# Opening in quarters: x and the first weight chunk loaded, split and multiplied in four pieces on two queues; the first squares later

## The chip, the cores and the metric

The kernel runs on one NeuronCore of a Trainium2 chip. The metric is the device time of one execution in microseconds (us). Five engines work beside each other, each through its own list in order, and wait for one another by semaphores: TensorE (PE, matmuls), VectorE (DVE), ScalarE (ACT), GpSimd (POOL) and SyncE (SP, which here only issues DMAs). ScalarE and GpSimd can issue DMAs too; those of SP and of ScalarE go through two different queues.

## What is computed

Two transformer blocks on 256 tokens of width 1024, in fp32, one after the other. What the change touches is the very first step, the first feed-forward layer with its norm:

```python
def rms_norm(x, g):
    xf = x.astype(jnp.float32)
    r = lax.rsqrt(jnp.mean(xf * xf, axis=-1, keepdims=True) + NORM_EPS)
    return (xf * r).astype(x.dtype) * g

def swiglu(u, w_in, w_out):
    a, b = jnp.split(u @ w_in, 2, axis=-1)
    return (jax.nn.silu(a) * b) @ w_out
...
x = x + FFN_RES_WEIGHT * swiglu(rms_norm(x, ffn1_norm), ffn1_w_in, ffn1_w_out)
```

`ffn1_w_in` is 1024 x 5632. Behind this layer follow two attention mixers, a second such layer, a gated embedding, a short convolution, two squared-ReLU layers and a sparse attention, none of which the change touches.

## The kernel before

x is kept transposed as `h`, 8 tiles of 128 features x 256 tokens. All weights come from memory as 198 chunks of 128 x 2048 fp32 (1 MB each), which stream through a ring of three buffers `raw`. An fp32 product is made of fp32r parts: ScalarE copies a chunk to its high part `w_hi` (L418), VectorE subtracts to get the low part `w_lo` (L816); both lie in `w_hl`. The same is done with the operand x: `gained_hi` (L446) multiplies by the norm's gain and makes `x_h`, `gained_lo` (L866) makes `x_l`. `wide` (L1561) then makes a product of two matmuls: high weights with both parts of x (512 columns, L1564) and low weights with the high part of x (256 columns, L1565). `thirds` (L1567) does the same with three matmuls of 256 columns.

A chunk of `ffn1_w_in` holds 128 columns of a and 128 of b for all 8 tiles of x, so it takes PE 16 such pairs. Chunk j makes tile j of the hidden layer in two PSUM banks, and three pairs of banks take turns. The norm's factor 1/rms is not on the operand; it is applied to the results. So the products need only the gain, and the factor is made beside them: `square` (L467) on ScalarE, `sum_tiles` (L883) on VectorE, `sum_squares` (L1678) on PE, `mean_square` (L839) on VectorE, `rsqrt` (L449: logarithm and exponential) on ScalarE, `newton` (L848) on VectorE into `r_sb`.

For each tile j (`ups`, L481 on ScalarE and L919 on VectorE): ScalarE copies the second half of the two banks to `second` (L479), VectorE adds it to the first half as `t_ab` (`whole_up`, L916), multiplies a by the factor (L931) and by b (L933), ScalarE makes the sigmoid (L496), VectorE the product `hid_f` (L938), ScalarE its high part in `hidden` (L498) and GpSimd its low part (L369). VectorE's L938 of tile j waits until GpSimd has read `hid_f` of tile j-1. Between these, `nxt(c)` splits chunk c+3 into the ring place that chunk c has left: on ScalarE when PE has used chunk c, on VectorE behind that. SP loads chunk c+3 into `raw` when `w_lo` of chunk c is written (L344). PE's chunk j waits for `w_lo` of chunk j, and from j = 3 on for the `whole_up` of tile j-3 (L1701), whose banks it overwrites.

The opening is written out by hand. x comes in two halves of 512 KB with the gain `par` between them on SP's queue; chunk 0 comes in halves, the first on ScalarE's queue, the second on SP's; chunks 1 and 2 and the constants follow on SP's. Chunk 0 is split and multiplied in quarters (`up` with `first`, L1627), chunk 1 in halves (`up_halves`, L1649). Before the first product PE runs `WARM` = 25 matmuls on `zeros`; it starts them when four of GpSimd's memsets are done (L1735). Every engine executes its list in the order in which the code is written.

```python
            pe.wait_ge(setup, 4)
            for n in range(WARM):
                mm(bank[:, SUMS, :], zeros[:, 0:P], zeros[:, :], start=True, stop=True)
            feed_forward("ffn1", x_hl, 1)
```

Of the kernel before, what the change touches and what calls it, by code (L numbers as in the profile page):

```python
# [14 lines left out]
F32 = mybir.dt.float32  # L15
# [3 lines left out]
ALU = mybir.AluOpType  # L19
# [21 lines left out]
WARM = 25  # L41
# [101 lines left out]
def program(nc, x_t, p_t, positions, weights, small, consts, rel_bias, bias_rows, bias_skew, out):  # L143
    with ExitStack() as ctx:
# [55 lines left out]
        x_in, first_in = [sem(f"x_in{j}") for j in range(2)], sem("first_in")  # L200
# [128 lines left out]
        def _(sp):  # L329
            sp.dma_start(h[:, 0:4, :], x_t[:, 0:4, :]).then_inc(x_in[0], 16)  # L330
            sp.dma_start(par[:, 0:KT], small[:, 0:KT]).then_inc(gain_in, 16)
            sp.dma_start(h[:, 4:8, :], x_t[:, 4:8, :]).then_inc(x_in[1], 16)
            sp.dma_start(raw[:, 0, CH // 2:CH], weights[0, :, CH // 2:CH]).then_inc(raw_landed[0], 16)
# [75 lines left out]
        def _(act):  # L409
# [132 lines left out]
            act.dma_start(raw[:, 0, 0:CH // 2], weights[0, :, 0:CH // 2]).then_inc(first_in, 16)  # L542
            nc.scalar.preload_act_table_set("natural_log_exp_and_others")
            for half in range(2):
                act.wait_ge(x_in[half], 16)
                if half == 0:
                    act.wait_ge(gain_in, 16)
                if half == 0:
                    for j in range(2):
                        gained_hi(x_h[:, 2 * j:2 * j + 2, :], h[:, 2 * j:2 * j + 2, :], "ffn1", 2 * j, 2 * j + 2)  # L550
                    act.wait_ge(first_in, 16)
                for q in range(2 * half, 2 * half + 2):
                    if half == 1:
                        gained_hi(x_h[:, 2 * q:2 * q + 2, :], h[:, 2 * q:2 * q + 2, :], "ffn1", 2 * q, 2 * q + 2)
                        act.wait_ge(raw_landed[0], 16)
                    a = slice(512 * q, 512 * q + 512)
                    nc.scalar.activation(w_hi[:, 0, a], raw[:, 0, a], ACT.Copy).then_inc(first_hi if q < 3 else hi_split, 1)
# [11 lines left out]
            rsqrt("ffn1", load=False)  # L569
            nc.scalar.preload_act_table_set("sigmoid_and_others")  # L570
# [3 lines left out]
            nxt(1)  # L574
            ups("ffn1")
# [233 lines left out]
        def _(dve):  # L809
# [109 lines left out]
            def ups(stage):  # L919
# [112 lines left out]
            for half in range(2):  # L1032
                dve.wait_ge(x_in[half], 16)
                if half == 0:
                    for j in range(2):
                        operand_piece("ffn1", x_h, x_l, j)
                for q in range(2 * half, 2 * half + 2):
                    if half == 1:
                        operand_piece("ffn1", x_h, x_l, q)
                    a = slice(512 * q, 512 * q + 512)  # L1040
                    if q < 3:
                        dve.wait_ge(first_hi, q + 1)
                    else:
                        dve.wait_ge(hi_split, 1)
                    V.tensor_tensor(w_lo[:, 0, a], raw[:, 0, a], w_hi[:, 0, a].bitcast(F32),
# [1309 lines left out]
```

## Time and profile before

| | |
|---|---|
| median of 3 runs | 1201.18 us (1198.7 to 1201.41) |
| span of the profiled execution | 1197.3 us |
| PE busy | 1187.6 us (99%) |
| VectorE busy | 867.8 us (72%) |
| ScalarE busy | 646.7 us (54%) |
| GpSimd busy | 220.6 us (18%) |
| DMA | 217.53 MB, mean 182 GB/s |
| chain that ended last | PE 96%, DVE 2%, ACT 1%, DMA 1% |

The profile shows one execution. Its span goes from the first to the last instruction; the profile does not give that execution's device time apart, and the median of the runs is 3.9 us above the span. Busy times overlap, so their shares don't add up. A start time in the timeline is counted from the span's start. Matmuls overlap in the array: the distance between the starts of two tells their cost, not the length of one.

### The profile page before, as it was taken

The numbers are of one execution on the slowest core, as the hardware profiler recorded it, in microseconds if no ns is written. First come the engines' busy times: TensorE is split into PE (matmuls) and PEld (weight loads), VectorE is DVE, ScalarE is ACT, GpSimd is POOL, SyncE is SP. The second block draws the span as 40 slices with busy tenths as digits, with TensorE's granted clock in tenths as the row PEclk, the third lists the DMA queues.
The fourth block names the chain that finished last, engine by engine and source line by source line (L and its number), as shares of the span: only waits on it lengthen the run. The fifth ranks groups of instructions, "written<-read, shape, count | busy, mean of one in ns | idle before, by whom it ended". The sixth has DMA issues, their size and how long they took to land.

```text
span 1197.3 us, 19531 instructions
## 1 busy us (share of the span) xinstructions
PE 1187.6 (99%) x7802; PEld 1060.7 (89%) x7802; DVE 867.8 (72%) x1199; ACT 646.7 (54%) x868; POOL 220.6 (18%) x110
## 2 busy tenths in 40 slices
PE   9999999999999999999999999999999999999997
PEld 6888889988899888888999988888899878888886
DVE  6877767788868877766788786655579777766553
ACT  6655554465654755545643555543446784555441
POOL 0443301000000344310000025510000340554000
PEclk9999999999999999999999999999999999999999
DMA  8655555953345555555545555555576305555540
GB/s 315 213 178 195 191 177 182 285 201 107 106 150 181 179 204 179 200 186 189 177 160 179 193 199 203 179 206 177 192 265 246 107 2 178 209 181 205 179 174 36
DMA packets 31569, 217.53 MB, mean 182 GB/s; under 512 B 3584, under 2 KB 3856, under 8 KB 6272
## 3 DMA queue, kind: packets, MB, share of 16 engines
q1 hardware_dynamic: 30000, 210.33, 50.4%
q0 software_dynamic: 1344, 5.53, 1.6%
q8 instruction: 59, 0.97, 0.3%
q10 hardware_dynamic: 144, 0.52, 0.1%
q14 instruction: 22, 0.18, 0.0%
HBM read 215.30 MB, written 4.22 MB: 183 GB/s over the span
## 4 chain that ended last, share of the span: by engine, by line
PE 96%; DVE 2%; ACT 1%; DMA 1%; issue 0%; POOL 0%; DVEq 0%; ACTq 0%; SPq 0%; POOLq 0%
PE bank L1564 42%; PE bank L1565 21%; PE bank L1557 8%; PE bank L1558 7%; PE bank L1559 7%; PE bank L1965 1%; PE bank L1673 1%; DVE w_hl L816 1%; PE bank L1737 1%; PE bank L1675 1%; PE bank L1674 1%; DMA raw<-weights 1%; ACT w_hl L418 0%; PE bank L1859 0%; PE bank L1842 0%; PE bank L1878 0%
## 5 line engine op out<-in xcount | busy, mean ns | idle before, releaser
L816 DVE TENSOR_TENSOR w_hl<-raw,w_hl 128x2048 fp32r<-128x2048 f32 x194 | 444.1, 2289 | 116.5 <-ACT w_hl L418 115.5
L418 ACT ACTIVATE w_hl<-raw 128x2048 fp32r<-128x2048 f32 x195 | 370.6, 1903 | 113.8 <-PE bank L1565 65.5
L1564 PE MATMUL bank<-x_hl,w_hl 128*128 128x512 f32 x908 | 316.5, 395 | 0.0
L1564 PE MATMUL bank<-hidden,w_hl 128*128 128x512 f32 x832 | 288.6, 394 | 0.0
L369 POOL TENSOR_TENSOR hidden<-hid_f,hidden 128x256 fp32r<-128x256 f32 (+1 forms) x76 | 189.5, 2493 | 519.8 <-ACT hidden L501 307.0
L1565 PE MATMUL bank<-x_hl,w_hl 128*128 128x256 f32 x908 | 251.9, 277 | 0.0
L1565 PE MATMUL bank<-hidden,w_hl 128*128 128x256 f32 x832 | 230.5, 277 | 0.0
L1564 PEld LDWEIGHTS bank<-x_hl,w_hl 128*128 128x128 f32 x908 | 170.3, 188 | 39.6
L1564 PEld LDWEIGHTS bank<-hidden,w_hl 128*128 128x128 f32 x832 | 156.0, 188 | 36.2
L1565 PEld LDWEIGHTS bank<-x_hl,w_hl 128*128 128x128 f32 x908 | 170.6, 188 | 0.1
L479 ACT ACTIVATE second<-bank 128x512 f32<-128x512 f32 (+1 forms) x107 | 57.2, 535 | 199.1 <-PE bank L1565 199.0
L1564 PE MATMUL bank<-y_hl,w_hl 128*128 128x512 f32 x448 | 156.8, 396 | 0.0
L1565 PEld LDWEIGHTS bank<-hidden,w_hl 128*128 128x128 f32 x832 | 156.2, 188 | 0.0
L1557 PE MATMUL bank<-x_hl,w_hl 128*128 128x256 f32 x528 | 151.1, 286 | 0.1
L1558 PE MATMUL bank<-x_hl,w_hl 128*128 128x256 f32 x528 | 149.3, 283 | 0.0
L1559 PE MATMUL bank<-x_hl,w_hl 128*128 128x256 f32 x528 | 149.3, 283 | 0.0
L1565 PE MATMUL bank<-y_hl,w_hl 128*128 128x256 f32 x448 | 124.5, 278 | 0.0
L1557 PEld LDWEIGHTS bank<-x_hl,w_hl 128*128 128x128 f32 x528 | 101.2, 192 | 2.1 <-issue 1.2
L1564 PEld LDWEIGHTS bank<-y_hl,w_hl 128*128 128x128 f32 x448 | 84.0, 188 | 20.0 <-issue 0.3
L1558 PEld LDWEIGHTS bank<-x_hl,w_hl 128*128 128x128 f32 x528 | 101.3, 192 | 0.1
L1559 PEld LDWEIGHTS bank<-x_hl,w_hl 128*128 128x128 f32 x528 | 101.2, 192 | 0.0
L916 DVE TENSOR_TENSOR t_ab<-bank,second 128x512 f32<-128x512 f32 x76 | 52.5, 690 | 64.3 <-ACT second L479 64.2
(385 smaller groups left out, 1536.0 us busy)
## 6 DMA issues: line engine op xcount, KB each, us to landing
raw<-weights SPq DMA_DIRECT2D x197, 1024.0 KB, 4.9
bias_skew<-bias_rows POOLq DMA_DIRECT2D x1, 3072.0 KB, 26.0
gate_or_bias<-bias_skew POOLq DMA_DIRECT2D x1, 2048.0 KB, 9.6
h<-x_t SPq DMA_DIRECT2D x2, 512.0 KB, 6.0
out_t<-out_g SPq DMA_DIRECT2D x4, 256.0 KB, 2.5
con<-consts SPq DMA_DIRECT2D x1, 769.5 KB, 13.3
raw<-weights ACTq DMA_DIRECT2D x1, 512.0 KB, 5.2
raw<-weights SPq DMA_DIRECT2D x1, 512.0 KB, 7.9
```

The costliest lines, as they stand in the source:

```text
L369: nc.gpsimd.tensor_tensor(hidden[:, at, 1, :], src, hidden[:, at, 0, :].bitcast(F32), ALU.subtract).then_inc(hid_lo, 1)
L418: nc.scalar.activation(dst, src, ACT.Copy).then_inc(hi_split, 1)
L479: nc.scalar.activation(dst, src, ACT.Copy).then_inc(second_out, 1)
L816: V.tensor_tensor(w_lo[:, s, :], raw[:, s, :], w_hi[:, s, :].bitcast(F32), ALU.subtract).then_inc(lo_split, 1)
L916: V.tensor_tensor(t_ab[:, :, :], bank[:, s:s + 2, 0:S], second[:, j % 2, :, :], ALU.add).then_inc(ab_ready, 1)
L1557: mm(out_, w_hi[:, s, c:c + m], x[:, 0, :], start=start, stop=False, **kw)
L1558: mm(out_, w_hi[:, s, c:c + m], x[:, 1, :], start=False, stop=False, **kw)
L1559: return mm(out_, w_lo[:, s, c:c + m], x[:, 0, :], start=False, stop=stop, **kw)
L1564: mm(out_, w_hi[:, s, c:c + m], x, start=start, stop=False, **kw)
L1565: return mm(out_[:, 0:S], w_lo[:, s, c:c + m], x[:, 0, :], start=False, stop=stop, **kw)
L1673: mm(o, a, wh, start=first and n == 0, stop=False, **kw)
L1674: mm(o, a, wl, start=False, stop=False, **kw)
```

## The change

- x is loaded in four pieces of 256 KB on SP's queue, and chunk 0 in four pieces of 256 KB on ScalarE's queue, behind the gain, which moves there too. Chunks 1 and 2 follow x on SP's queue as before.
- ScalarE and VectorE work on x and chunk 0 piece by piece: the quarter of x, then the quarter of the chunk. Before, the first two pieces of x came ahead of the first quarter of the chunk.
- GpSimd sets `zeros` first. PE waits for that alone, runs 13 instead of 25 matmuls on zeros, and then waits for the other memsets.
- ScalarE makes the high part of chunk 2 ahead of the four squares, and both `second` of tile 1 and the high part of chunk 4 ahead of the logarithm, the exponential and the table load.
- VectorE makes the low part of chunk 2 ahead of the sums, and `whole_up` of tile 0 and the low parts of chunks 3 and 4 ahead of the mean square and `newton`. Chunk 4's low part stood behind `whole_up` of tile 1 before.
- PE sums the squares behind chunk 2 instead of chunk 1.
- `thirds` is gone; all pairs are `wide`.

VectorE's list from the sums to the second `whole_up`, before (`sq` are squares and sums, `t_m` the mean square, the three rows behind it up to `r_sb` are `newton`, `w_hl` of 128x2048 is a chunk's low part):

```order
L879 TENSOR_TENSOR sq<-sq 128x512 x3
L881 TENSOR_TENSOR sq<-sq 128x256
L816 TENSOR_TENSOR w_hl<-raw,w_hl 128x2048
L842 TENSOR_SCALAR t_m<-bank 128x256
L916 TENSOR_TENSOR t_ab<-bank,second 128x512
L816 TENSOR_TENSOR w_hl<-raw,w_hl 128x2048
L851 TENSOR_TENSOR t_a<-t_exp 128x256
L852 SCALAR_TENSOR_TENSOR t_a<-t_a,t_m 128x256
L854 SCALAR_TENSOR_TENSOR r_sb<-t_a,t_exp 128x256
```

The same place after the change:

```order
L810 TENSOR_TENSOR w_hl<-raw,w_hl 128x2048
L873 TENSOR_TENSOR sq<-sq 128x512 x3
L875 TENSOR_TENSOR sq<-sq 128x256
L910 TENSOR_TENSOR t_ab<-bank,second 128x512
L810 TENSOR_TENSOR w_hl<-raw,w_hl 128x2048 x2
L836 TENSOR_SCALAR t_m<-bank 128x256
L845 TENSOR_TENSOR t_a<-t_exp 128x256
L846 SCALAR_TENSOR_TENSOR t_a<-t_a,t_m 128x256
L848 SCALAR_TENSOR_TENSOR r_sb<-t_a,t_exp 128x256
```

Chunk 2's low part moved ahead of the sums, and those of chunks 3 and 4 now both stand ahead of the mean square.

ScalarE's list from chunk 1's high part to the first sigmoid, before (`second` is the copy from the banks, `t_a<-t_m` the logarithm, `t_exp<-t_a` behind it the exponential):

```order
L561 ACTIVATE w_hl<-raw 128x1024 x2
L468 ACTIVATE sq<-h 128x512 x4
L418 ACTIVATE w_hl<-raw 128x2048
L479 ACTIVATE second<-bank 128x512
L418 ACTIVATE w_hl<-raw 128x2048
L453 ACTIVATE t_a<-t_m 128x256
L454 ACTIVATE t_exp<-t_a 128x256
L570 ACT_TABLE_LOAD
L479 ACTIVATE second<-bank 128x512
L418 ACTIVATE w_hl<-raw 128x2048
```

And after:

```order
L555 ACTIVATE w_hl<-raw 128x1024 x2
L416 ACTIVATE w_hl<-raw 128x2048
L466 ACTIVATE sq<-h 128x512 x4
L477 ACTIVATE second<-bank 128x512
L416 ACTIVATE w_hl<-raw 128x2048
L477 ACTIVATE second<-bank 128x512
L416 ACTIVATE w_hl<-raw 128x2048
L451 ACTIVATE t_a<-t_m 128x256
L452 ACTIVATE t_exp<-t_a 128x256
L568 ACT_TABLE_LOAD
```

The logarithm and what hangs on it moved behind the copy of tile 1 and the high part of chunk 4.

```diff
-WARM = 25
+WARM = 13
...
         def _(sp):
-            sp.dma_start(h[:, 0:4, :], x_t[:, 0:4, :]).then_inc(x_in[0], 16)
-            sp.dma_start(par[:, 0:KT], small[:, 0:KT]).then_inc(gain_in, 16)
-            sp.dma_start(h[:, 4:8, :], x_t[:, 4:8, :]).then_inc(x_in[1], 16)
-            sp.dma_start(raw[:, 0, CH // 2:CH], weights[0, :, CH // 2:CH]).then_inc(raw_landed[0], 16)
+            for j in range(4):
+                sp.dma_start(h[:, 2 * j:2 * j + 2, :], x_t[:, 2 * j:2 * j + 2, :]).then_inc(x_in[j], 16)
...
-            for n, (t, value) in enumerate(((ones[:, :], 1.0), (zeros[:, :], 0.0), (v_pad[:, :, :], 0.0),
+            for n, (t, value) in enumerate(((zeros[:, :], 0.0), (ones[:, :], 1.0), (v_pad[:, :, :], 0.0),
...
-            act.dma_start(raw[:, 0, 0:CH // 2], weights[0, :, 0:CH // 2]).then_inc(first_in, 16)
+            act.dma_start(par[:, 0:KT], small[:, 0:KT]).then_inc(gain_in, 16)
+            for q in range(4):
+                a = slice(512 * q, 512 * q + 512)
+                act.dma_start(raw[:, 0, a], weights[0, :, a]).then_inc(first_in[q] if q < 3 else raw_landed[0], 16)
...
+            act.wait_ge(gain_in, 16)
+            for q in range(4):
+                act.wait_ge(x_in[q], 16)
+                gained_hi(x_h[:, 2 * q:2 * q + 2, :], h[:, 2 * q:2 * q + 2, :], "ffn1", 2 * q, 2 * q + 2)
+                act.wait_ge(first_in[q] if q < 3 else raw_landed[0], 16)
+                a = slice(512 * q, 512 * q + 512)
+                nc.scalar.activation(w_hi[:, 0, a], raw[:, 0, a], ACT.Copy).then_inc(first_hi if q < 3 else hi_split, 1)
...
+            split(2, 2, 1)
             for j in range(4):
                 square(j)
-            split(2, 2, 1)
...
             nxt(0)
-            rsqrt("ffn1", load=False)
-            nc.scalar.preload_act_table_set("sigmoid_and_others")
...
             nxt(1)
+            rsqrt("ffn1", load=False)
+            nc.scalar.preload_act_table_set("sigmoid_and_others")
...
-                    if c0 + j == 1:
-                        nxt(1)
...
+            split(2, 3)
             sum_tiles("ffn1")
-            split(2, 3)
-            mean_square("ffn1", bank[:, SUMS, 0:S])
             whole_up("ffn1", 0)
             nxt(0)
+            nxt(1)
+            mean_square("ffn1", bank[:, SUMS, 0:S])
             newton("ffn1", r_sb[:, :])
...
-                        form = thirds if half == 1 and t == 0 else wide
...
-                    if j == (1 if stage == "ffn1" else 0):
+                    if j == (2 if stage == "ffn1" else 0):
                         sum_squares(norm_no)
...
-            pe.wait_ge(setup, 4)
+            pe.wait_ge(setup, 1)
             for n in range(WARM):
                 mm(bank[:, SUMS, :], zeros[:, 0:P], zeros[:, :], start=True, stop=True)
+            pe.wait_ge(setup, 5)
```

## Rows read from the trace of the kernel before

**Rows 1.** The page: the span, and PE's busy time, share and instructions.

```profile
span 1197.3 us, 19531 instructions
...
PE 1187.6 (99%) x7802; PEld 1060.7 (89%) x7802; DVE 867.8 (72%) x1199; ACT 646.7 (54%) x868; POOL 220.6 (18%) x110
```

**Rows 2.** Timeline of the opening: start us, length us, engine, line, count [idle before <-releaser].

```profile
1.02 0.53 POOL L357 MEMSET zeros<- 128x512 bf16 x1
...
2.35 8.47 PE L1737 MATMUL bank<-zeros 128*128 128x512 bf16 x25 [2.35 <-POOL relb L357]
...
7.88 2.94 PE L1737 MATMUL bank<-zeros 128*128 128x512 bf16 x12
...
10.47 0.58 PE L1564 MATMUL bank<-x_hl,w_hl 128*128 128x512 f32 x1
```

**Rows 3.** SP's timeline, then issues of x, chunks 1, 1 and 2, 4: median to landing.

```profile
0.76 0.40 SPq L330 DMA_DIRECT2D h<-x_t  x1
...
2.62 1.00 SPq L335 DMA_DIRECT2D raw<-weights  x2
...
16.21 0.34 SPq L344 DMA_DIRECT2D raw<-weights  x1
...
h<-x_t SPq DMA_DIRECT2D x1, 512.0 KB, 5.1
...
raw<-weights SPq DMA_DIRECT2D x1, 1024.0 KB, 9.9
...
raw<-weights SPq DMA_DIRECT2D x2, 1024.0 KB, 10.9
...
raw<-weights SPq DMA_DIRECT2D x1, 1024.0 KB, 7.8
```

**Rows 4.** ScalarE's timeline: high parts of chunks 1 and 3, and the exponential.

```profile
12.58 2.01 ACT L561 ACTIVATE w_hl<-raw 128x1024 fp32r<-128x1024 f32 x2 [0.51 <-DMA raw<-weights]
...
20.80 1.92 ACT L418 ACTIVATE w_hl<-raw 128x2048 fp32r<-128x2048 f32 x1 [1.83 <-DMA raw<-weights]
...
23.36 0.42 ACT L454 ACTIVATE t_exp<-t_a 128x256 f32<-128x256 f32 x1
```

**Rows 5.** VectorE's timeline, from the last piece of x to chunk 6's low part.

```profile
11.58 0.88 DVE L866 SCALAR_TENSOR_TENSOR x_hl<-h,par,x_hl 128x256 fp32r<-128x256 f32 x2
...
13.68 2.36 DVE L1053 TENSOR_TENSOR w_hl<-raw,w_hl 128x1024 fp32r<-128x1024 f32 x2 [0.61 <-ACT w_hl L561]
15.95 2.14 DVE L879 TENSOR_TENSOR sq<-sq 128x512 f32<-128x512 f32 x3
...
22.45 0.42 DVE L842 TENSOR_SCALAR t_m<-bank 128x256 f32<-128x256 f32 x1 [1.64 <-PE bank L1681]
...
25.59 0.42 DVE L851 TENSOR_TENSOR t_a<-t_exp 128x256 f32<-128x256 f32 x1
...
28.29 0.69 DVE L916 TENSOR_TENSOR t_ab<-bank,second 128x512 f32<-128x512 f32 x1
...
32.60 0.42 DVE L938 TENSOR_TENSOR hid_f<-t_b,t_exp 128x256 f32<-128x256 f32 x1
...
36.45 2.29 DVE L816 TENSOR_TENSOR w_hl<-raw,w_hl 128x2048 fp32r<-128x2048 f32 x1
...
40.69 2.29 DVE L816 TENSOR_TENSOR w_hl<-raw,w_hl 128x2048 fp32r<-128x2048 f32 x1
```

**Rows 6.** PE's timeline: the first matmuls of chunks 1 and 5.

```profile
16.21 0.39 PE L1564 MATMUL bank<-x_hl,w_hl 128*128 128x512 f32 x1
...
38.90 0.40 PE L1564 MATMUL bank<-x_hl,w_hl 128*128 128x512 f32 x1
```

**Rows 7.** Tile hidden, 20 to 60 us: GpSimd's low part, ns min/median/max.

```profile
L369 POOL TENSOR_TENSOR hidden<-hid_f,hidden x8: 738/2274/2795, 29.0 to 59.4; 128x256 fp32r<-128x256 f32 x8
```

**Rows 8.** Windows at the tail: PE, PEld, DVE, ACT, POOL busy, granted clock, DMA.

```profile
1189.00:1191.00 2.00, 1.28 (x7) 0.66 (x7) 0.64 (x4) 0.86 (x4) 0.00 (x0) 1.00 0.00 0
...
1192.00:1193.00 1.00, 0.00 (x0) 0.00 (x0) 1.00 (x2) 0.00 (x0) 0.00 (x0) 0.84 0.00 0
```

More of the change, by code:

```diff
@@ L199, in program @@
         half_hi = sem("half_hi")
-        x_in, first_in = [sem(f"x_in{j}") for j in range(2)], sem("first_in")
+        x_in, first_in = [sem(f"x_in{j}") for j in range(4)], [sem(f"first_in{j}") for j in range(3)]
         gain_in, small_in, con_in, relb_in, pos_in, p_in = (
@@ L539, in gained_out @@
                 nc.scalar.activation(out_g[:, o, :], h[:, o, :], ACT.Copy, scale=col("final", o)).then_inc(gained, 1)
-            act.dma_start(raw[:, 0, 0:CH // 2], weights[0, :, 0:CH // 2]).then_inc(first_in, 16)
+            act.dma_start(par[:, 0:KT], small[:, 0:KT]).then_inc(gain_in, 16)
+            for q in range(4):
+                a = slice(512 * q, 512 * q + 512)
+                act.dma_start(raw[:, 0, a], weights[0, :, a]).then_inc(first_in[q] if q < 3 else raw_landed[0], 16)
             nc.scalar.preload_act_table_set("natural_log_exp_and_others")
[L544 to L557, printed above, removed]
+            act.wait_ge(gain_in, 16)
[5 more added lines that the diff above has]
+                nc.scalar.activation(w_hi[:, 0, a], raw[:, 0, a], ACT.Copy).then_inc(first_hi if q < 3 else hi_split, 1)
             act.wait_ge(raw_landed[1], 16)
@@ L1031, in _ @@
             dve.wait_ge(gain_in, 16)
[L1032 to L1045, printed above, removed]
-                                    ALU.subtract).then_inc(first_lo if q < 3 else lo_split, 1)
+            for q in range(4):
+                dve.wait_ge(x_in[q], 16)
+                operand_piece("ffn1", x_h, x_l, q)
+                a = slice(512 * q, 512 * q + 512)
+                if q < 3:
+                    dve.wait_ge(first_hi, q + 1)
+                else:
+                    dve.wait_ge(hi_split, 1)
+                V.tensor_tensor(w_lo[:, 0, a], raw[:, 0, a], w_hi[:, 0, a].bitcast(F32),
+                                ALU.subtract).then_inc(first_lo if q < 3 else lo_split, 1)
             for q in range(2):
@@ L1565, in wide @@
                 return mm(out_[:, 0:S], w_lo[:, s, c:c + m], x[:, 0, :], start=False, stop=stop, **kw)
-            def thirds(out_, s, c, m, x, start, stop):
-                kw = dict(skip_group_check=True)
-                mm(out_[:, 0:S], w_hi[:, s, c:c + m], x[:, 0, :], start=start, stop=False, **kw)
-                mm(out_[:, S:2 * S], w_hi[:, s, c:c + m], x[:, 1, :], start=False, stop=False, **kw)
-                return mm(out_[:, 0:S], w_lo[:, s, c:c + m], x[:, 0, :], start=False, stop=stop, **kw)
             def arrived(count):
@@ L1656, in up_halves @@
                     for t in range(2):
-                        form = thirds if half == 1 and t == 0 else wide
                         for k in range(KT // 2 * half, KT // 2 * (half + 1)):
-                            last = form(bank[:, 2 * slot + t, :], 1, k * 256 + t * P, P, x[:, k, :, :], k == 0,
+                            last = wide(bank[:, 2 * slot + t, :], 1, k * 256 + t * P, P, x[:, k, :, :], k == 0,
                                         k == KT - 1)
```

## The prediction

> **What bounds the kernel now.** I read the page first: TensorE (PE) is busy 1187.6 us of a span of 1197.3 us [rows 1]. The 9.7 us without it are the first 2.35 us and the tail, so from the first filler matmul on the kernel is one unbroken row of matmuls. Then I read the opening in the timeline. 25 matmuls on zeros run from 2.35 us, 0.425 us apart until about 8.3 us and 0.216 us apart after it (13 start before 7.88 us, 12 in the 2.59 us to 10.47 us); the first product starts at 10.47 us [rows 2]. The reader is to see that the fillers run right up to it: PE's start waits for their end. Chunk 1 starts at 16.21 us and chunk 5 at 38.90 us [rows 6], each 16 pairs of 0.346 us, or 5.54 us. So a microsecond saved at the start is saved at the end, if nothing between takes it back. What could take it is in rows 5: chunk 5's low part is written from 36.45 us for 2.29 us, to 38.74 us, and PE needs it at 38.90 us [rows 5, 6]. There the cover is 0.16 us.
>
> **The change, start of PE.** The memset of the zeros takes 0.53 us from 1.02 us, and PE now waits for two more behind it, until 2.35 us [rows 2]. As the first memset it ends at about 1.3 us, so PE starts at about 1.4 us. 13 fillers at the slow pace take 5.5 us and end at 6.9 us. The 12 removed ones are worth 2.6 to 5.1 us of PE.
>
> **First pieces.** The first 512 KB of x land 5.1 us after their issue at 0.76 us, at 5.9 us [rows 3]. A quarter holds half as much on each of the two queues: no row shows when it lands. It is bounded by 5.9 us above and by about 3.3 us below (half of the 5.1 us after the issue); I take 4.6 us, the middle. VectorE needs 0.88 us for the x of a piece and, at 2.36 us for two halves of a chunk, 0.6 us for its weights [rows 5]; ScalarE, ahead of it, takes much the same. That puts the first product at 4.6 + 0.9 (ScalarE, x) + 0.9 + 0.7 = 7.1 us, just behind the fillers. VectorE's 1.5 us for a piece is a little more than PE's 1.38, so PE ends chunk 0 at about 7.1 + 3 x 1.5 + 1.4 = 13.0 us, against 16.21 us. The five issues on ScalarE's queue (0.4 us each, as SP's [rows 3]) push its table load from 1.2 to about 2.9 us; it ends before x is there and costs nothing. If the pieces come 1.5 us later than I take, chunk 0 still ends by 14.5 us, and the next step hides it.
>
> **Chunk 1 keeps most of it.** Chunk 1's 1024 KB are issued behind all of the x pieces and land 9.9 us after 2.62 us, at 12.5 us [rows 3]. The same bytes go ahead of them after the change. Its first half is split on ScalarE at 12.58 us and on VectorE at 13.68 us, and stands at 14.90 us [rows 4, 5]. PE then starts chunk 1 at 14.9 us instead of 16.21 us: of 3.2 us gained before it, 1.3 are left and 1.9 are a pause. The landing can be earlier: chunk 2 lands 2.5 us behind chunk 1 (two issues, mean 10.9 us, the first 9.9), so 1 MB takes 2.5 us, and from the first megabyte at 5.9 us the third could be in at 10.9 us [rows 3]. Above, I allow 1 us of delay, since the pieces are smaller. The form with three matmuls of 256 goes; it has the same columns and hides in the pause.
>
> The DMA page of the Trainium skill (DMA: Bandwidth & Descriptors, section Bandwidth) advises batches of at least 1 MiB and gives 2.0 us fixed for a DMA on GpSimd's path. If these added up, an estimate from the page would be 3 x 2.0 = 6 us more for four pieces. The trace disagrees: chunk 2, a DMA of its own, lands 2.5 us behind chunk 1, which is what its 1 MB takes at 420 GB/s, so nothing fixed stands between two DMAs of one queue [rows 3].
>
> **The reordered norm takes it back.** Chunk 2's split now goes ahead of the squares, and both next splits (chunks 3 and 4) ahead of the mean square and the factor. Follow VectorE. Chunk 2 lands at 15.0 us, its split takes 1.9 on ScalarE and 2.3 on VectorE: 19.3 us, and PE wants it at 14.9 + 5.5 = 20.4 us. The sums take 2.14 us for three and about 0.4 for the last [rows 5] and the first whole_up 0.6: 22.4 us. Chunk 3's high part is made from 20.80 us, when it has landed, to 22.7 us [rows 4]; its low part stands at 25.0 us. Chunk 4 is issued when chunk 1's split is over, at 16.21 us, and lands 7.8 us later, at 24.0 us [rows 3]. Now nobody waits for it; after the change VectorE does: high part 24.1 to 26.0, low part 26.05 to 28.3 us. Only then the mean square. From its start at 22.45 us to the end of ScalarE's exponential at 23.78 us are 1.3 us now [rows 4, 5], so Newton's step starts at 28.3 + 1.3 = 29.6 us, against 25.59 us. From there to the second whole_up are 2.7 us (25.59 to 28.29), and 0.7 us for itself: 33.0 us.
>
> PE: chunk 2 from 20.4, the sum of squares (now behind chunk 2) 0.4, chunk 3 from 26.4, end 31.9 us. Chunk 4 writes the banks that the second whole_up reads, so it waits until 33.0 us: a pause of 1.1 us; before it started at about 33.35 us. So here 0.3 us of the gain is left.
>
> Then chunk 5. Its high part stands in ScalarE's queue behind the gate of tile 1. That gate's last product (L938) starts at 32.60 us now, and chunk 5's low part ends at 38.74 us: 6.1 us of hid_f, hidden, second, high part, sigmoid, hid_f, low part, with no slack but waits on each other [rows 5]. After the change whole_up ends at 33.0, two products of 0.46 us and a sigmoid follow: 34.0 us at the earliest. But L938 also waits for GpSimd's low part of tile 0, which starts at about 32.9 us and takes 0.74 to 2.8 us [rows 7]; at the short end it costs nothing, at the long one L938 starts at 35.7 us. VectorE is idle for part of that stretch, so I take a value nearer the short end, 34.5 us. Chunk 5 is ready at 34.5 + 6.1 = 40.6 us (40.1 to 41.8) against a start at 38.90 us now. PE, free at 38.6 us, waits 2.0 us: **1.7 us lost** (1.2 to 2.9). After that a tile costs VectorE and ScalarE 4.2 us (36.45 to 40.69, [rows 5]) against PE's 5.5, so nothing more is lost, and PE runs without a gap to the end as before; the loss passes through. By pauses it is the same: -1.3 (start) + 1.05 + 2.0 = +1.75. The span would be 1199.0 us. Between the span and the median of the three runs lie 3.9 us, which the change doesn't touch: 1201.18 + 1.7 = 1202.9 us.
>
> **Rivals.** (1) *The clock falls in a pause*: slower. PE now never stops for more than a fraction of a microsecond before the end; there, with 1.28 us busy of 2.00 us and little after, the granted clock falls during 1192 to 1193 us [rows 8]. The pauses of 1.9 us (13.0 to 14.9) and 2.0 us (38.6 to 40.6) are about as thin. Each fall would run PE at 1.2 instead of 2.4 GHz for a while. The only low stretch that the trace shows is 2.35 to about 8.3 us, which costs half of 5.9, so at most 3.0 us; I take 2.2 us for one fall: 1202.9 + 2.2 = 1205.1 us, up to 1208 for two. [...] For it: the tail. Against: there the gaps came after thin work, here full work stands on both sides.
>
> TensorE: Matmul & The Clock Gate of the Trainium skill (section HAM oscillation) says that waits for DMA between bursts bring the lower clock back. By that rule this rival has more than a small chance; the row of the tail agrees in kind.
>
> (2) *Loads land earlier*, because two queues share them from the start: everything up to 1.6 us earlier. VectorE then does chunks 3 and 4 back to back behind its sums (22.4 + 2.2 + 2.2 = 26.8 us), 1.4 us earlier than above, and chunk 5 is ready at 39.2 us: +0.3 us, 1201.5 us.
>
> (3) *The gain survives*: if L938 of tile 1 does not wait and chunk 4's landing is no longer last, chunk 5 would have to be ready by 37.6 us, 3 us sooner than my chain: 1201.2 - 1.3 = 1199.9 us. Only the 6.1 us taken from rows full of waits speaks for it.
>
> (4) *It doesn't do what it says*: the quarter pieces land at 5.9 us or later, PE idles behind 13 slow fillers and is still at the low clock. Chunk 0 then ends as late as 16 us and the first 1.3 us go too, but chunk 5's chain doesn't hang on that: again 1202.9 us, or 1 us more.
>
> **Numbers.** Forecast 0.52, (1) 0.20, (2) 0.16, (3) 0.07, (4) 0.05. The forecast's own range is 1202.0 to 1204.1 us. With the three runs' spread of 2.7 us in mind, 8 in 10 lie between 1199.9 and 1205.6 us. 0.3% is 3.6 us, about what a measurement can tell here. Faster by more needs both ends of the loads and a short chain: 0.02. Slower by more is two thirds of (1) and a little of the rest: 0.15. Within: 0.83.
>
> **What would show it.** In the new profile: fillers from 1.4 us, first product near 7 us, a pause before chunk 1 that ends at chunk 1's split near 14.9 us; the mean square near 28.3 us; PE waiting for t_ab at 33 us and for chunk 5's low part until about 40.6 us; from there the same distances as now. Wrong it would be if chunk 5 starts before 38.9 us, if the mean square starts before 26 us, or if matmuls 0.69 us a pair stand behind a pause.

## The result and the profile after

| | before | after |
|---|---|---|
| median of the runs | 1199.37 us (1197.99 to 1203.93, 8 runs) | 1204.6 us (1201.78 to 1206.61, 8 runs) |
| span of the profiled execution | 1197.3 us | 1201.5 us |
| PE busy | 1187.6 us | 1187.5 us |
| chunk 0, 1, 5 start | 10.47, 16.21, 38.90 us | 7.66, 17.41, 41.88 us |

Both kernels were timed on the same chip; the ratio is 1.0032 with an interval of 1.002 to 1.0044. The change costs 5.2 us by the medians, 3.8 us by the ratio (2.4 to 5.3) and 4.2 us by the spans of the two profiled executions. That of after took 1203.27 us, 1.8 us more than its span. Three single slow runs (4148.77 us of e7_best, 3016.35 and 1665.42 us of before beside e10_pause and e12_no_pause) are left out of every number below.

The page of after, its span and busy times, beside [rows 1]:

```profile
span 1201.5 us, 19505 instructions
...
PE 1187.5 (99%) x7786; PEld 1061.5 (88%) x7786; DVE 868.4 (72%) x1199; ACT 646.7 (54%) x868; POOL 218.6 (18%) x110
```

The waits of PE in after (us in total, times, longest):

```profile
PE bank L1552 <- DVE w_hl L1032: 4.0, 4, 1.5
PE bank L1552 <- DVE w_hl L810: 1.4, 1, 1.4
PE bank L1717 <- POOL zeros L355: 1.3, 1, 1.3
```

PE's timeline of after: the four quarters of chunk 0, chunk 1, the sum of squares, chunk 4 and chunk 5, beside [rows 2, 6]:

```profile
7.66 0.47 PE L1552 MATMUL bank<-x_hl,w_hl 128*128 128x512 f32 x1 [0.68 <-DVE w_hl L1032]
...
10.47 0.47 PE L1552 MATMUL bank<-x_hl,w_hl 128*128 128x512 f32 x1 [1.17 <-DVE w_hl L1032]
...
12.77 0.47 PE L1552 MATMUL bank<-x_hl,w_hl 128*128 128x512 f32 x1 [0.65 <-DVE w_hl L1032]
...
15.94 0.47 PE L1552 MATMUL bank<-x_hl,w_hl 128*128 128x512 f32 x1 [1.52 <-DVE w_hl L1032]
...
17.41 0.42 PE L1552 MATMUL bank<-x_hl,w_hl 128*128 128x512 f32 x1
...
28.73 0.59 PE L1661 MATMUL bank<-sq,ones 128*128 128x256 f32 x2
...
34.72 0.39 PE L1552 MATMUL bank<-x_hl,w_hl 128*128 128x512 f32 x1
...
41.88 0.50 PE L1552 MATMUL bank<-x_hl,w_hl 128*128 128x512 f32 x1 [1.45 <-DVE w_hl L810]
```

PE starts its products 2.8 us sooner than before and waits in front of each of the four quarters, so that chunk 1 starts 1.2 us later (17.41 against 16.21 us). Ahead of chunk 4, at 34.72 us, it doesn't wait. It waits once more, for chunk 5's low part, which starts 3.0 us later than before (41.88 against 38.90 us).

ScalarE's timeline of after: the quarters of chunk 0 (L551), and the logarithm, beside [rows 4]:

```profile
5.79 0.61 ACT L551 ACTIVATE w_hl<-raw 128x512 fp32r<-128x512 f32 x1
...
8.97 0.63 ACT L551 ACTIVATE w_hl<-raw 128x512 fp32r<-128x512 f32 x1 [1.77 <-DMA raw<-weights]
...
11.27 0.63 ACT L551 ACTIVATE w_hl<-raw 128x512 fp32r<-128x512 f32 x1 [0.87 <-DMA raw<-weights]
...
14.44 0.63 ACT L551 ACTIVATE w_hl<-raw 128x512 fp32r<-128x512 f32 x1 [1.74 <-DMA raw<-weights]
...
29.82 0.42 ACT L451 ACTIVATE t_a<-t_m 128x256 f32<-128x256 f32 x1 [4.13 <-DVE t_m L836]
```

Three of four quarters are waited for by ScalarE itself: the releaser is the DMA. VectorE's timeline of after: low parts of chunks 3 and 4, mean square, the second whole_up, the factor times tile 1, hid_f of tile 1 and chunk 5's low part, beside [rows 5]:

```profile
24.13 4.48 DVE L810 TENSOR_TENSOR w_hl<-raw,w_hl 128x2048 fp32r<-128x2048 f32 x2
29.36 0.42 DVE L836 TENSOR_SCALAR t_m<-bank 128x256 f32<-128x256 f32 x1 [0.75 <-PE bank L1661]
...
33.43 0.68 DVE L910 TENSOR_TENSOR t_ab<-bank,second 128x512 f32<-128x512 f32 x1
34.15 0.99 DVE L923 TENSOR_TENSOR t_a<-t_ab,r_sb 128x256 f32<-128x256 f32 x1
...
35.69 0.43 DVE L930 TENSOR_TENSOR hid_f<-t_b,t_exp 128x256 f32<-128x256 f32 x1
...
39.53 2.29 DVE L810 TENSOR_TENSOR w_hl<-raw,w_hl 128x2048 fp32r<-128x2048 f32 x1
```

From chunk 5 to the end of the span are 1158.4 us before and 1159.6 us after. About as much as the 1.2 us between them is lost in a dip of the clock near 946 us, beside smaller shifts of both signs elsewhere. The windows of after show it (PE, PEld, DVE, ACT, POOL busy, then the granted clock, DMA share, GB/s):

```profile
946.00:947.00 1.00, 1.00 (x7) 0.35 (x4) 0.97 (x3) 0.30 (x1) 0.02 (x1) 0.50 1.02 434
947.00:948.00 1.00, 1.00 (x5) 1.00 (x6) 0.96 (x5) 0.40 (x1) 0.00 (x0) 0.50 0.57 238
```

Before, the clock is 1.00 in each microsecond from 944 to 949 us. Here it is 0.50, or 1.2 of 2.4 GHz. The same dip stands in the profiled executions of e1, e3, e4, e11, e12 and e13 below and not in those of e2, e5, e7, e8, e9 and e10, with unlike openings among both. So it seems to go with the execution and not with the change; one profile of each kernel can't prove that. What the change itself costs in this pair of profiles is then the 3.0 us at chunk 5.

### The profile page after: what moved, and what is told of

Same layout as the page of the kernel before. It is cut to its first block, busy times and chain, and to the rows that moved or that the text cites. A ratio compares the mean times of both kernels' runs of the same rounds, so it can differ in the third digit from the quotient of the medians.

```text
span 1201.5 us, 19505 instructions
## 1 busy us (share of the span) xinstructions
PE 1187.5 (99%) x7786; PEld 1061.5 (88%) x7786; DVE 868.4 (72%) x1199; ACT 646.7 (54%) x868; POOL 218.6 (18%) x110
## 4 chain that ended last, share of the span: by engine, by line
PE 95%; DVE 2%; DMA 2%; ACT 1%; issue 0%; ACTq 0%; DVEq 0%; SPq 0%
PE bank L1552 41%; PE bank L1553 21%; PE bank L1545 8%; PE bank L1546 8%; PE bank L1547 8%; DMA raw<-weights 2%; PE bank L1946 1%; PE bank L1653 1%; DVE w_hl L810 1%; PE bank L1654 1%; PE bank L1655 1%; ACT w_hl L416 0%; PE bank L1840 0%; PE bank L1823 0%; PE bank L1859 0%; PE bank L1993 0%
```

## The experiments

Two questions lead. Which part of the change makes the 3.0 us, and why do medians differ by more than that? The ratio in each row is to runs of before on the same chip; the starts are of one profiled execution each.

| kernel | median us (lowest to highest) | ratio, interval | chunk 1, chunk 5 at us |
|---|---|---|---|
| e1_norm_only | 1203.66 (1201.12 to 1206.48) | 1.003, 1.0016 to 1.0045 | 15.87, 40.79 |
| e2_open_only | 1202.43 (1200.29 to 1206.78) | 1.0014, 0.9998 to 1.0031 | 16.93, 39.88 |
| e3_fill13 | 1201.96 (1200.14 to 1203.93) | 1.001, 0.9995 to 1.0025 | 17.13, 39.83 |
| e4_hold | 1206.85 (1205.47 to 1209.59) | 1.0053, 1.0032 to 1.0074 | 17.10, 43.28 |
| e11_halves | 1204.39 (1201.41 to 1206.96) | 1.0032, 1.0019 to 1.0045 | 17.15, 41.38 |
| e9_after_early5 | 1204.76 (1203.57 to 1206.03) | 1.0039, 1.0023 to 1.0054 | 18.06, 41.11 |
| e5_early5 | 1199.33 (1198.26 to 1199.65) | 0.9989, 0.9978 to 1.0001 | 15.67, 38.42 |
| e8_no_early5 | 1201.32 (1198.55 to 1204.09) | 1.0017, 1.0005 to 1.0029 | 14.62, 38.12 |
| e7_best | 1198.25 (1197.16 to 1200.72) | 0.999, 0.9979 to 1.0 | 14.64, 37.39 |
| e10_pause | 1202.86 (1199.76 to 1203.58) | 1.0015, 1.0004 to 1.0026 | 15.64, 38.97 |
| e12_no_pause | 1198.95 (1198.68 to 1199.66) | 0.9988, 0.9975 to 1.0002 | 15.40, 38.16 |
| e13_pause10 | 1202.40 (1201.71 to 1204.28) | 1.0014, 1.0001 to 1.0027 | 16.06, 38.75 |

A start read from one profile has a spread of its own. Before, e1, e5, e10, e12 and e13 have the same opening, and chunk 1 starts anywhere from 15.40 to 16.21 us; in after, e2 and e9, which share the other one, from 16.93 to 18.06 us. Before is the latest of its six. Differences below 1 us between two profiles should be read with that in mind.

### The norm's new order alone (e1_norm_only)

The kernel before, with the late norm of the change and nothing of its opening:

```diff
+            split(2, 2, 1)
             for j in range(4):
                 square(j)
-            split(2, 2, 1)
...
-            rsqrt("ffn1", load=False)
-            nc.scalar.preload_act_table_set("sigmoid_and_others")
...
             nxt(1)
+            rsqrt("ffn1", load=False)
+            nc.scalar.preload_act_table_set("sigmoid_and_others")
...
+            sum_tiles("ffn1")
...
+            nxt(1)
+            mean_square("ffn1", bank[:, SUMS, 0:S])
```

> The kernel before with the reordered norm alone (chunk 2's split ahead of the squares, chunks 3 and 4 split ahead of the mean square, the sum of squares behind chunk 2); opening as before. Theory A (the chain from chunk 4's landing over the mean square, Newton's step and the second whole_up to chunk 5's low part is what costs): chunk 1 starts at 16.2 us as before, the mean square starts near 28.3 us instead of 22.45, chunk 5 starts at 40.6 us instead of 38.90, and the time is 1.7 us longer than before. Theory B (the late landing of the quarters alone costs): chunk 5 at 38.9 us and the time of before.

VectorE's timeline of e1_norm_only, the mean square and hid_f of tile 1:

```profile
28.29 0.42 DVE L842 TENSOR_SCALAR t_m<-bank 128x256 f32<-128x256 f32 x1
...
34.61 0.43 DVE L936 TENSOR_TENSOR hid_f<-t_b,t_exp 128x256 f32<-128x256 f32 x1
```

PE's timeline of it, the first matmul of chunk 5:

```profile
40.79 0.50 PE L1563 MATMUL bank<-x_hl,w_hl 128*128 128x512 f32 x1 [1.81 <-DVE w_hl L816]
```

The forecast of the chain was 28.3, 34.5 and 40.6 us: the chain is as worked out, and its price at chunk 5 is 1.9 us against before. Behind the pause of 1.81 us the granted clock fell, as windows of e1_norm_only show:

```profile
42.00:43.00 1.00, 1.00 (x5) 0.81 (x4) 0.91 (x3) 0.44 (x2) 0.00 (x0) 0.50 0.77 197
43.00:44.00 1.00, 1.00 (x4) 0.82 (x4) 1.00 (x1) 1.00 (x3) 0.70 (x1) 0.50 0.98 418
```

Chunk 6 started at 48.02 us, 7.23 us behind chunk 5 instead of 5.55, so the fall cost another 1.7 us there. That is rival (1), at its place and near its price (2.2 us), in this execution; in the profile of after, behind a pause of 1.45 us, it did not happen.

### The opening alone (e2_open_only)

The changed kernel, with the norm in its old order (the diff above, reversed).

> The changed kernel with the norm's order of before: quarters on two queues, 13 fillers, but squares, mean square and Newton's step where they were. Theory A: chunk 0 ends late (chunk 1 near 17.4 us, as in the changed kernel), but chunk 5 starts within 0.3 us of chunk 1's delay, near 40.1 us, 1.2 us longer than before. Theory B: all of the changed kernel's loss, chunk 5 at 41.9 us, 3 us longer than before.

Chunk 1 started at 16.93 us and chunk 5 at 39.88 us, 1.0 us later than before and not 1.3 us earlier. With the 1.9 us of e1_norm_only that makes the 3.0 us of after; that it fits to 0.1 us is chance, given the spread above. So the opening, which the prediction had put at a gain that the norm takes back, is a loss of its own.

### Who delays the quarters (e4_hold, e11_halves)

In e4_hold SyncE issues chunks 1 and 2 only when three quarters of chunk 0 are there:

```diff
+            sp.wait_ge(first_in[2], 16)
             for c in range(1, RING):
```

> The changed kernel, but SP issues chunks 1 and 2 only when the third quarter of chunk 0 has landed. Theory D (chunks 1 and 2 on SP's queue take the bandwidth from chunk 0's quarters on ScalarE's queue): the quarters land by about 5.5, 7, 8.5 and 9.5 us instead of 5.7, 8.95, 11.2 and 14.4, the first product stays near 7.7 us and chunk 0 is done near 12 us; chunk 1, issued near 8.5 us, lands at 12.5 us or later and its product starts near 15 us. Rival E (2 KB pieces are slow by themselves): the last quarter lands after 12 us here too. Either way chunk 5 can't start before about 40.6 us because of the norm's order, so 1.2 us less than the changed kernel at best.

ScalarE's timeline of e4_hold (quarters 3 and 4 of chunk 0, then chunk 1):

```profile
10.12 0.62 ACT L552 ACTIVATE w_hl<-raw 128x512 fp32r<-128x512 f32 x1
...
11.45 0.62 ACT L552 ACTIVATE w_hl<-raw 128x512 fp32r<-128x512 f32 x1
14.73 2.01 ACT L556 ACTIVATE w_hl<-raw 128x1024 fp32r<-128x1024 f32 x2 [2.66 <-DMA raw<-weights]
```

The last two quarters are there before ScalarE comes to them; quarter 4 is worked on 3.0 us sooner than in after. Only quarter 2 is about as late as in after (8.79 against 8.97 us); what holds it up is not shown. So chunks 1 and 2 on SP's queue were what delayed the last quarters. But chunk 1 then lands late itself (14.7 us), chunk 1 starts at 17.10 us behind a pause of 2.1 us, the clock falls behind it (0.50 from 20 to 21 us), and the kernel is the worst of all.

e11_halves takes the other way: after, with x and chunk 0 in two DMAs of 512 KB each on the same two queues, and the work still in quarters.

```diff
-            for j in range(4):
-                sp.dma_start(h[:, 2 * j:2 * j + 2, :], x_t[:, 2 * j:2 * j + 2, :]).then_inc(x_in[j], 16)
+            for j in range(2):
+                sp.dma_start(h[:, 4 * j:4 * j + 4, :], x_t[:, 4 * j:4 * j + 4, :]).then_inc(x_in[j], 16)
...
-            for q in range(4):
-                a = slice(512 * q, 512 * q + 512)
+            for q in range(2):
+                a = slice(1024 * q, 1024 * q + 1024)
```

> The changed kernel, but with x in two pieces of 512 KB on SP's queue and chunk 0 in two pieces of 512 KB on ScalarE's queue; the work is still done in quarters. Theory D (chunks 1 and 2 behind x take the bandwidth from chunk 0 on the other queue): the first half of chunk 0 lands near 6 us, the second half near 12 us or later. Rival E (pieces with 2 KB rows are slow, nothing else): the second half lands by 10 us. In the changed kernel the quarters land at 5.7, 8.95, 11.2 and 14.4 us; with chunks 1 and 2 held back they did at 5.8, 8.8, 9.8 and 10.45 us.

The second half is there at about 12.2 us, where the last quarter of after came at 14.4; theory D had it near 12 us or later, rival E by 10 us. The first half, at 8.4 us, is later than a quarter (5.8 us), and PE waits 4.3 us behind its 13 fillers; the clock falls behind that wait too. Chunk 1 starts at 17.15 us: no gain.

The DMA views tell how the two queues share (queue, packets, MB, share of the 16 engines' time; q1 is SP's, q10 ScalarE's). After, from 10.5 to 13.2 us:

```profile
q1 hardware_dynamic: 136, 0.98, 86.2%
q10 hardware_dynamic: 96, 0.17, 16.1%
```

e11_halves, from 9 to 12 us:

```profile
q1 hardware_dynamic: 128, 0.92, 72.4%
q10 hardware_dynamic: 102, 0.35, 28.8%
```

Packets of the two queues are not far apart in number in both (136 and 96, 128 and 102), bytes are: a packet of ScalarE's queue has 1.8 KB in after and 3.4 KB in e11_halves, one of SP's 7.2 KB in both. A row of a quarter is 512 fp32 long, one of a half 1024, one of a whole chunk 2048. So the queues seem to take turns by packet, and a load of short rows beside one of long rows gets the small share: of some 420 GB/s, the last quarter (0.26 MB from 11.27 to 14.44 us) got 83. The section Queues, rings and completion order of the Trainium skill's page DMA: Bandwidth & Descriptors says that each DMA engine serves its queues in turn, a packet at a time; these rows agree in the main, with 1.3 to 1.4 packets of SP's queue to one of ScalarE's.

### Fewer fillers (e3_fill13)

Before, with zeros set first, 13 fillers and the other memsets waited for behind them:

```diff
-WARM = 25
+WARM = 13
...
-            pe.wait_ge(setup, 4)
+            pe.wait_ge(setup, 1)
             for n in range(WARM):
                 mm(bank[:, SUMS, :], zeros[:, 0:P], zeros[:, :], start=True, stop=True)
+            pe.wait_ge(setup, 5)
```

> The kernel before with the zeros first, PE starting on them alone, and 13 instead of 25 fillers; nothing else. Theory A (0.16 us of cover at chunk 5, so an earlier start is not kept): the first product starts near 9.6 us instead of 10.47, chunk 1 near 15.3, but chunk 5 no earlier than 38.7 us; gain 0.2 us at most. Rival C (the chain to chunk 5 moves along with PE): chunk 5 at 38.0 us and 0.9 us gained.

PE's timeline of e3_fill13, its first product:

```profile
9.94 0.74 PE L1564 MATMUL bank<-x_hl,w_hl 128*128 128x512 f32 x1 [3.06 <-DVE w_hl L1045]
```

Two windows behind it:

```profile
10.00:11.00 1.00, 1.00 (x3) 0.90 (x4) 1.00 (x3) 1.00 (x4) 0.00 (x0) 0.50 0.99 418
11.00:12.00 1.00, 1.00 (x5) 0.81 (x5) 1.00 (x3) 1.00 (x3) 0.00 (x0) 0.50 1.01 426
```

Without the last fillers the first product starts 0.5 us sooner (9.94 against 10.47 us), behind 3.06 us of nothing, and then runs at half the clock: chunk 1 starts 0.9 us later than before. Neither theory A nor rival C had that fall of the clock. The fillers of before that cover the wait for the first weights are not waste.

### Chunk 5's chain (e5_early5, e8_no_early5, e7_best, e9_after_early5)

Chunk 5's split is the gate through which a gain of the opening has to pass. The edit of e5_early5 on before: ScalarE copies tile 2's second half and makes chunk 5's high part ahead of tile 1's sigmoid, VectorE makes its low part right behind tile 1's hid_f.

```diff
-                    if c0 + j > 1:
+                    if c0 + j > 2:
...
+                    if c0 + j == 1:
+                        act.wait_ge(chunk_used, 3)
+                        act.wait_ge(ab_ready, 1)
+                        second_half(stage, 2, second[:, 0, :, :], bank[:, 2 * SLOTS[2]:2 * SLOTS[2] + 2, S:2 * S])
+                        nxt(2)
...
+                    if c0 + j == 1:
+                        nxt(2)
-                    if j < n - 1 and c0 + j > 1:
+                    if j < n - 1 and c0 + j > 2:
```

> The kernel before with that early split of chunk 5 and nothing else. Chunk 5 is ready near 36.5 us instead of 38.73, PE starts it at 38.9 us as before, since PE itself was the bound: no change of time. It shows the price of the edit alone.

The low part of chunk 5 ended at 34.76 us instead of 38.73, with 3.7 us of cover where before had 0.16. The median moved by no more than the measurement tells (ratio 0.9989), but the runs drew together: all 12 within 1.4 us, while those of before beside them spread over 6.9 us.

e8_no_early5 and e7_best share another opening on before: zeros first, 20 fillers, and the work on x and chunk 0 a quarter at a time, with the two halves' DMAs where before has them. e7_best has e5's edit as well.

> The kernel before with its halves of x and chunk 0, but the zeros first, PE starting on them alone with 20 fillers, and each quarter of x followed at once by the quarter of chunk 0. The first product starts near 8.8 us (high and low parts of one quarter less ahead of it), chunk 1 at 14.9 us when its first half is split. Theory A (cover of 0.16 us at chunk 5): chunk 5 not before 38.5 us, 0.4 us gained at most. Rival C: the start's 1.3 us are kept, chunk 5 at 37.6 us. [...]

> The same opening with the early split of chunk 5. Theory A: chunk 5 is ready by 36.5 us and PE starts it at 37.6 us, 1.3 us ahead of the kernel before, and keeps that: 1.3 us faster than before, 1198 us. If this is no faster than the kernel without the early split, the cover at chunk 5 was not what took the start's gain.

In both chunk 1 starts at 14.6 us, 1.6 us sooner than before and 0.8 us sooner than the earliest of the kernels with before's opening. In e8_no_early5 PE then waits for chunk 5's low part, which starts at 38.12 us:

```profile
38.12 0.50 PE L1558 MATMUL bank<-x_hl,w_hl 128*128 128x512 f32 x1 [0.54 <-DVE w_hl L814]
```

That is 0.8 us sooner than before, between theory A (38.5) and rival C (37.6). Its profile is the fastest of its runs; the median, 1201.32 us, is longer than that of before, and the next part shows why that may be. In e7_best nothing waits there, chunk 5 starts at 37.39 us, 1.5 us sooner than before, and the span is 1195.3 us. Its median of 1198.25 us is the lowest of all, though the interval of its ratio ends at 1.0, so that a gain over before is not shown.

> The changed kernel, but chunk 5's split is taken out of the end of the chain: ScalarE makes tile 2's second and chunk 5's high part ahead of tile 1's sigmoid, VectorE its low part right behind tile 1's product (L930). Theory A (the wait before chunk 5 is this chain): the mean square stays at 29.4 us and the second whole_up at 33.4, but chunk 5 is ready near 39 us and PE starts it when chunk 4 ends, at 40.3 us instead of 41.88: 1.6 us less than the changed kernel. Rival: something else (chunk 5's landing, GpSimd) is late too, and PE still waits until 41 us or more.

On after, e5's edit takes the wait at chunk 5 away (chunk 5 starts at 41.11 us, on PE's own row, and a wait of 0.73 us is left at chunk 6), yet the median stays. From chunk 1 to chunk 5 are 23.05 us, 1.4 us less than in after: the gain of theory A (1.6) is there. But in that execution the opening was 0.65 us later (chunk 1 at 18.06 us), and PE ran at the slower of the two paces that the next part is about.

### A pause that costs more than itself (e10_pause, e12_no_pause, e13_pause10)

The run times of before lie in two clusters: of 20 beside e10_pause, 11 from 1198.43 to 1199.37 us and 9 from 1201.37 to 1202.76 us. Profiles show the like: in a stretch of matmuls alone, from 60 to 160 us, with the clock granted in full, PE starts 579 matmuls in some executions and 568 in others. The windows of e5_early5 and of e2_open_only:

```profile
60.00:160.00 100.00, 100.00 (x579) 87.44 (x578) 72.42 (x86) 53.90 (x67) 33.03 (x15) 1.00 0.54 190
```

```profile
60.00:160.00 100.00, 100.00 (x568) 86.77 (x567) 71.33 (x84) 53.26 (x67) 34.02 (x15) 1.00 0.53 184
```

Chunks are 5.55 us apart at the one pace and 5.65 at the other, to about 235 us, which makes some 3 us. Before and after were profiled at 579. Is it chance, or does a pause set it? e10_pause is e5_early5, with PE made to wait ahead of chunk 5 for a product of tile 3; e12_no_pause has the same wait for tile 2, which is there long before; e13_pause10 has none at chunk 5, but waits ahead of chunk 10 for ScalarE's copy of tile 9.

```diff
+                    if c0 + j == 5:
+                        pe.wait_ge(sig_in, 4)
```

> The kernel before with the early split of chunk 5 (which has no pause in its row of products), but PE's chunk 5 also waits for the gate operand of the fourth tile: a pause of about 0.5 us before chunk 5, and nothing else. Theory F (a pause in the row of products can leave PE at a slower cadence, 176.7 ns from matmul to matmul instead of 173.3, until the end of the layer near 190 us): about half of the executions are 0.5 us longer than without the pause, the others 3.6 us. Rival G (the cadence is chance of each execution, whatever the pauses): the times form the same single group as without the pause, 0.5 us higher.

> The control of e10_pause: the same early split of chunk 5 and the same added wait of TensorE ahead of chunk 5, but for VectorE's product of tile 2 in place of tile 3, which is there some 3 us earlier; so the instruction stands in PE's list and nothing is waited for. Theory F (a pause in the row of products leaves PE in the pace of 176.7 ns from matmul to matmul instead of 173.3): as e5_early5, all runs within 1198.2 to 1200.0 us, chunk 5 at 38.4 us, 579 matmuls from 60 to 160 us. The rival, that the added wait itself or the chance of an execution made e10_pause slow: runs between 1201 and 1204 us as there.

> The early split of chunk 5, no wait ahead of it, and a pause at another place: ahead of chunk 10 (66.2 us) TensorE waits for ScalarE's copy of tile 9, whose banks are full only when chunk 9 ends. The copy takes 0.6 us, so the pause is some 0.7 to 0.8 us, with all operands long there. Theory F: a wait of 0.7 us costs 0.8 us where it stands, and in most executions another 2.5 us or so from there to about 235 us: median about 1202.6 us, in two groups near 1200.1 and 1202.8; in a slow execution 579 matmuls' pace until 66 us and 568 per 100 us behind it (chunks 5.55 us apart before, 5.65 us after). The rival, that only something about chunk 5 or the opening makes executions slow: median 1200.1 us, all runs within 1199 to 1201 us.

The windows of e10_pause, then of e12_no_pause:

```profile
60.00:160.00 100.00, 100.00 (x568) 86.73 (x567) 70.60 (x84) 53.70 (x67) 33.92 (x15) 1.00 0.53 181
```

```profile
60.00:160.00 100.00, 100.00 (x579) 87.48 (x578) 72.41 (x87) 53.88 (x67) 32.75 (x15) 1.00 0.54 190
```

The windows of e13_pause10, one before and two behind the start of chunk 10:

```profile
45.00:66.00 21.00, 21.00 (x123) 18.36 (x122) 18.07 (x21) 12.90 (x17) 10.28 (x5) 1.00 0.68 245
68.00:89.00 21.00, 21.00 (x121) 18.18 (x120) 14.99 (x20) 11.17 (x15) 7.48 (x4) 1.00 0.56 197
89.00:110.00 21.00, 21.00 (x121) 18.23 (x120) 15.06 (x19) 12.07 (x15) 8.41 (x4) 1.00 0.51 177
```

PE's timeline of it, the first matmul of chunk 10:

```profile
67.42 0.47 PE L1571 MATMUL bank<-x_hl,w_hl 128*128 128x512 f32 x1 [0.78 <-ACT second L479]
```

With the pause of 0.48 us at chunk 5, 9 of 12 runs take 1202.0 to 1203.6 us; with the same wait that does not wait, all 11 take 1198.7 to 1199.7 us. With a pause of 0.78 us at chunk 10 all 11 take over 1201.7 us, and in its profile the pace changes at the pause: 123 matmuls in 21 us ahead of it, 121 behind. (e12_no_pause and e13_pause10 ran on one chip; e10_pause ran on another, where the median of before was 1199.37 against 1199.41 us.) So a pause of half a microsecond at these two places costs itself and, in most executions, some 3 us more.

A pause is neither needed nor enough, though. PE's timeline of e2_open_only shows no wait from chunk 1 to chunk 5; its rows are the starts of chunk 1, of the sum of squares and of chunks 3, 4 and 5:

```profile
16.93 0.40 PE L1553 MATMUL bank<-x_hl,w_hl 128*128 128x512 f32 x1
...
22.49 0.59 PE L1662 MATMUL bank<-sq,ones 128*128 128x256 f32 x2
...
28.57 0.40 PE L1553 MATMUL bank<-x_hl,w_hl 128*128 128x512 f32 x1
...
34.23 0.40 PE L1553 MATMUL bank<-x_hl,w_hl 128*128 128x512 f32 x1
...
39.88 0.40 PE L1553 MATMUL bank<-x_hl,w_hl 128*128 128x512 f32 x1
```

Chunk 1 takes 5.56 us, chunks 3 and 4 take 5.66 and 5.65: PE fell into the slower pace at the sum of squares. In after it came back to the faster one there: chunks 1 and 2 take 5.67 and 5.65 us, chunks behind the sum 5.55, behind the pause of 1.45 us at chunk 5 too. The profiles of e1, e4 and e8, with pauses of 0.54 to 2.1 us, are at 579 as well. In e3_fill13 PE fell into the slower pace at chunk 5 without a pause; the rows are the starts of chunks 3 to 6:

```profile
28.73 0.39 PE L1564 MATMUL bank<-x_hl,w_hl 128*128 128x512 f32 x1
...
34.27 0.39 PE L1564 MATMUL bank<-x_hl,w_hl 128*128 128x512 f32 x1
...
39.83 0.41 PE L1564 MATMUL bank<-x_hl,w_hl 128*128 128x512 f32 x1
...
45.48 0.40 PE L1564 MATMUL bank<-x_hl,w_hl 128*128 128x512 f32 x1
```

Chunk 5's low part ended at 39.67 us there, 0.16 us ahead of PE, the same cover as in before. That may be where the slower cluster of before comes from, which e5_early5 and e12_no_pause, with 3.7 us of cover, don't have; no execution of before in that cluster was profiled to show it. What in the chip makes the two paces stays open; the granted clock is 1.00 in both.

## Why the prediction was right, and where it wasn't

The forecast was 1202.9 us, within 0.3% of before, and 1204.6 us came, 0.32% above before by the ratio, just past that bound. It lies outside the forecast's own range (1202.0 to 1204.1) and inside the wider one (1199.9 to 1205.6). That it came this near is in part luck, since two errors worked against each other: the base was 1.8 us too high, the cost 3.5 us too low by the medians (1.7 forecast, 5.2 measured; 3.8 by the ratio). Of the mechanism, the chain of the norm to chunk 5 was right; the gain of the opening was not.

- **Start of PE: right.** Fillers from 1.33 us (forecast 1.4), ended by about 7.0.
- **First pieces: wrong.** The first product came at 7.66 us (7.1). The first x landed at 4.4 us (4.6), but the first weights at 5.7 us; and the five issues took until 3.7 us, so that the table load ended at 4.96 us, 0.4 us behind the gain's landing. As the weights came last, that cost 0.1 us at most. But chunk 0 ended at 17.4 us and not at 13.0: the step took one landing for the first piece and let the others follow at the pace of VectorE, 1.5 us. They came 3.2, 2.3 and 3.2 us apart. It said that pieces 1.5 us late would be hidden; the last was later than that.
- **Chunk 1 keeps most of it: wrong.** Forecast 14.9 us, measured 17.41. The premise that the same bytes go ahead of chunk 1 as before was false: of chunk 0, what was on SP's queue moved to ScalarE's, and chunk 1, issued right behind x at 2.62 us, landed 10.6 us later, at 13.2 us, ahead of the last quarter. It was 0.7 us late; chunk 0 was what held PE up, and chunk 1's split had to wait for that of the last quarter until 14.98 us. Rival (4), late pieces, is of this kind, though it took them all to come at 5.9 us or later together, and not one by one; it was given 0.05. Rival (2), earlier loads, had it the wrong way round: the second queue made the quarters late and chunk 1 no earlier.
- **The weighing of the page was beside the point.** A fixed cost between the DMAs of one queue is indeed not seen in [rows 3]. The rule that bore on this change is another of the Trainium skill's page DMA: Bandwidth & Descriptors, the one on how two queues share an engine, cited at e11_halves. (The 2.0 us stand in that page's section Anatomy of one DMA, not in the one that the prediction names.)
- **The reordered norm: right,** and to 0.2 us in e1_norm_only. GpSimd's part took its short end (0.74 us at 34.12 us). In after the mean square came at 29.36 us, not 28.3, since PE's sum, behind the late chunk 2, ended last there: the releaser of L836 is PE. The forecast's pause of 1.1 us ahead of chunk 4 didn't come, since PE was there only at 34.72 us, behind the second whole_up. The sentence on rival (4), that chunk 5's chain does not hang on the opening, or by 1 us, was near: it hung on it by 1.3 us (41.88 against 40.6 us).
- **Rival (1): right in kind, but not in after's profile.** Falls of the clock stand behind pauses of 1.8, 2.1, 3.1 and 4.3 us (e1_norm_only, e4_hold, e3_fill13, e11_halves), none behind those of after (up to 1.5 us). The price at chunk 5 was 1.7 us (e1_norm_only) against 2.2.
- **Between the span and the time: wrong.** The 3.9 us compared a profiled execution of one cluster with a median in the other. Of one execution the difference is 1.8 us.
- **Not foreseen at all:** the two paces. The two fastest runs of after, 1201.78 and 1202.12 us, lie about 3 us above the middle of before's lower cluster, which is the shift at chunk 5; the other six lie 1.2 to 4.5 us higher. The slower pace (3 us) and falls of the clock (1.2 to 1.7 us) are of that size; that they are what makes these six longer is argued from size alone. Which run had which can't be told, since one execution of each kernel was profiled.

## What to carry to other kernels

Before a load is cut in pieces and moved to a second queue, look at what the first queue carries beside it: a load of short rows beside one of long rows gets the small share of the bandwidth, and a piece that is needed now can be overtaken by a chunk that is needed later. When a chain has 0.16 us of cover somewhere behind the opening, part of a gain ahead of it is lost there and a delay goes through, so widen that place first (chunk 5 at 38.12 us in e8_no_early5, at 37.39 in e7_best). A short pause of TensorE can cost more than itself; compare the distances between matmuls behind it, not the pause alone, and compare clusters of run times before medians. And profile a kernel twice before reading a few tenths of a microsecond from it.

## What the runs showed of the hardware

- TensorE has two paces in a row of the same matmuls at full granted clock: 579 or 568 starts in 100 us (5.55 or 5.65 us for 32 matmuls). By their times, a pause of 0.48 us left it in the slower one in 9 of 12 runs, one of 0.78 us in all of 11, and the runs of e5_early5 and e12_no_pause, without a pause, were all 23 in the faster. It also changed without a pause: to the slower one at the sum of squares in e2_open_only and at chunk 5 in e3_fill13, to the faster one at the sum of squares in after.
- Two hardware queues share the DMA engines nearer by packets than by bytes: 136 to 96 packets, 0.98 to 0.17 MB in 2.7 us; with rows twice as long on ScalarE's queue 128 to 102 packets, 0.92 to 0.35 MB in 3 us.
- VectorE's product of 0.42 us took 0.99 us at 34.15 us, beside GpSimd's low part, which ran from 34.12 us for 0.74 us:

```profile
34.12 0.74 POOL L367 TENSOR_TENSOR hidden<-hid_f,hidden 128x256 fp32r<-128x256 f32 x1 [31.47 <-ACT hidden L496]
```

No experiment here tests that the one delays the other.
